# A hybrid attention and state-space layer: first q panel tiles in the row norm, convolution steps one at a time, panel loads at the fifth tile

## The reference

```python
xn = _rmsnorm(x, norm1_w)
proj = xn @ w_in
q, k, v, f_raw, z, xbc, dt_raw, g_att, g_ssm = _split_proj(proj)
...
xbc_c, conv_new = _causal_conv(xbc, conv_past, conv_w, conv_b)   # width 4, then silu
y, h_new = _ssd(xh, dt, A, Bm, Cm, h0)
...
merged = (jax.nn.sigmoid(g_att) * (att.reshape(b, T, ATT_WIDTH) @ w_pa)
          + jax.nn.sigmoid(g_ssm) * (y_ssm @ w_pb))
x = x + merged @ w_out
h = _rmsnorm(x, norm2_w)
x = x + jnp.square(jax.nn.relu(h @ w_up)) @ w_down
```

## Time and profile before

| | |
|---|---|
| median of 3 runs | 2886.76 us |
| profiled execution | 2885.89 us |
| its span | 2884.1 us |
| PE busy | 2737.1 us (95%), 18754 matmuls |
| DVE, ACT, POOL busy | 1577.2, 1022.4, 405.7 us |
| stages (us from the start) | norm to 41, q, k, v to 366, attention from about 404 to 1315, SSD and gates from 1330, branches from 1702, output norm from 2010, MLP from 2131 |

### The profile page before, as it was taken

The page is one execution under the profiler, slowest core; times in us unless marked ns, Lnnn a source line. Parts: engine busy times, 40 slices in busy tenths (PEclk is TensorE's granted clock), DMA queues, the critical chain, the costliest instruction groups (busy, mean ns, idle before and its releaser), DMA issues. The chain is left out here.

```text
span 2884.1 us, 47789 instructions
## 1 busy us (share of the span) xinstructions
PE 2737.1 (95%) x18754; PEld 2658.0 (92%) x18754; DVE 1577.2 (55%) x2867; ACT 1022.4 (35%) x2353; POOL 405.7 (14%) x475
## 2 busy tenths in 40 slices
PE   6998979999999999997999989998989999999999
PEld 5997978989999889887999979998989999999999
DVE  4336337656566565565898864464373444434434
ACT  4223336556666655653434331121231111111110
POOL 0000012212122222222555520000000000000000
PEclk8999999999999999998999999999989999999999
DMA  3222232132232222215888873343221111111112
GB/s 115 90 90 53 79 90 91 43 101 76 67 108 76 66 93 58 84 63 140 205 194 214 201 203 121 112 134 128 65 99 58 45 44 45 44 45 44 48 67 96
DMA packets 334448, 273.31 MB, mean 95 GB/s; under 512 B 95952, under 2 KB 311632, under 8 KB 334096
## 3 DMA queue, kind: packets, MB, share of 16 engines
q1 hardware_dynamic: 334224, 270.25, 32.9%
HBM read 197.90 MB, written 72.28 MB: 94 GB/s over the span
## 5 line engine op out<-in xcount | busy, mean ns | idle before, releaser
L411 PE MATMUL banks<-w_hi,xn_hi 128*128 128x256 f32 x1440 | 407.8, 287 | 8.7 <-DVEq L368 5.0
L411 PE MATMUL banks<-w_lo,xn_hi 128*128 128x256 f32 x1440 | 405.5, 286 | 0.0
L414 PE MATMUL banks<-xn_hi,w_hi 128*128 128x352 f32 x1152 | 379.5, 329 | 0.7 <-ACT att_xs L986 0.7
L414 PE MATMUL banks<-xn_hi,w_lo 128*128 128x352 f32 x1152 | 378.7, 329 | 0.0
L414 PE MATMUL banks<-xn_lo,w_hi 128*128 128x352 f32 x1152 | 378.2, 328 | 0.0
L411 PE MATMUL banks<-w_hi,xn_lo 128*128 128x256 f32 x1280 | 366.3, 286 | 0.0
L411 PEld LDWEIGHTS banks<-w_hi,xn_hi 128*128 128x128 f32 x1440 | 276.7, 192 | 10.6 <-DVEq L368 5.1
L411 PEld LDWEIGHTS banks<-w_lo,xn_hi 128*128 128x128 f32 x1440 | 276.6, 192 | 0.2
L1704 PE MATMUL banks<-h_hi,w_hi 128*128 128x352 f32 x768 | 248.8, 324 | 1.9 <-DVEq L1625 1.9
L1704 PE MATMUL banks<-h_lo,w_hi 128*128 128x352 f32 x768 | 248.6, 324 | 0.0
L1704 PE MATMUL banks<-mlp_uhi,w_hi 128*128 128x352 f32 x768 | 248.6, 324 | 0.0
(11 more groups left out here) (293 smaller groups left out, 6160.8 us busy)
## 6 DMA issues: line engine op xcount, KB each, us to landing
w_raw<-in_w_in SPq DMA_DIRECT2D x44, 1024.0 KB, 5.5
scratch_xbc<-att_co SPq DMA_DIRECT2D x32, 512.0 KB, 2.6
ssd_ab<-scratch_acum SPq DMA_DIRECT2D x64, 256.0 KB, 6.0
br_g<-scratch_gates SPq DMA_DIRECT2D x72, 176.0 KB, 2.8
scratch_gates<-hand_tanh SPq DMA_DIRECT2D x48, 176.0 KB, 5.4
scratch_z<-att_z_stage SPq DMA_DIRECT2D x64, 128.0 KB, 1.9
ssd_xbc<-scratch_xbc SPq DMA_DIRECT2D x64, 128.0 KB, 3.4
ssd_xbc<-scratch_xbc SPq DMA_DIRECT2D x128, 64.0 KB, 3.7
```

The lines of the kernel that those rows point to most:

```text
L411: ins = self.nc.tensor.matmul(self.bank(n, P, PW), x[:, k, t * P:(t + 1) * P], w[:, k, :], start=first, stop=end)
L414: ins = self.nc.tensor.matmul(self.bank(n, P, TT), w[:, k, m * P:(m + 1) * P], x[:, k, r * TT:(r + 1) * TT], start=first, stop=end)
```

## The change

Four things are changed.

1. In `norm_split`, the q panel is loaded before row tile 3, its high part is made by ACT ahead of the sixth squares and its low part by DVE ahead of the seventh round. PE multiplies the first eight tiles of that panel there (`multiply`), each behind the transposes of the tile three further on, and keeps the results in banks 4 to 7 (`held_bank`, two tiles a bank). SP loads the k panel behind it. `project_qkv` begins with the ninth tile; ACT reads the eight held ones from their banks.
2. The load of panel j + 2 is issued after the fifth tile (`t == 4`), in all streams.
3. The low parts of the panels are made by DVE in the attention stage as well; POOL keeps only the doubling copies.
4. The convolution's five instructions of a block are put in a queue (`due`), and `step` runs one of them at given places in a unit; what is left of a block four tiles after its end is run then. ACT's tanh and the stores of the block come one tile later. `share[2]` is (2, 2, 4) where it was (2, 3, 3).

```diff
+HELD = 8
+def held_bank(core, n, rows, cols):
+    b = (5, 6, 7, 4)[n // 2]
+    return core.banks[0:rows, b, (n % 2) * PW:(n % 2) * PW + cols]
...
             for t in range(1, NT):
+                if t == W_AT:
+                    sp.dma_start(panel(core.raw), following...).then_inc(p_loaded, 16)
                 sp.dma_start(rows[:, t, :], srcs[0][t * P:(t + 1) * P, :]).then_inc(loaded[t], 16)
...
+            sp.wait_ge(p_split, 2)
+            sp.dma_start(panel(core.raw), second...).then_inc(next_loaded, 16)
+            sp.wait_ge(next_loaded, 16)
...
-                if t == NT + 1:
+                if t == W_AT + 2:
                     act.wait_ge(p_loaded, 16)
                     nc.scalar.activation(core.whi[0][:], core.raw[:], ACT.Copy).then_inc(p_split, 1)
...
+                if t == W_AT + 3:
+                    dve.wait_ge(p_split, 1)
+                    nc.vector.tensor_tensor(core.wlo[0][:], core.raw[:], core.whi[0][:].bitcast(F32), ALU.subtract).then_inc(p_split, 1)
...
+            def multiply(t):
+                if t == 0:
+                    pe.wait_ge(p_split, 2)
+                pe.wait_ge(lo_made, 2 * t + 2)
+                passes = [(x, w, k) for k in range(KB) for x, w in ((hi, whi), (hi, wlo), (lo, whi))]
...
+                for m in behind(t):          # [t - 3] for t from 3 to 8
+                    multiply(m)
+            for m in range(NT - LAG, HELD):  # 6, 7
+                multiply(m)
+            pe.wait_ge(multiplied, HELD)
...
     def sp(self, sp, i, n, last):
         j, t = self.tiles[n]
-        if t == 5:
+        if t == 4:
             self.load(sp, i, j + 2, last)
...
-        if 1 <= t < 5 and not self.low_on_pool:
-            self.split_lo(dve, self.nc.vector, i, j + 1, t - 1)
+        if 1 <= t < 5:
+            self.split_lo(dve, i, j + 1, t - 1)
...
+        if i == 0 and n < self.held:
+            if n == 0:
+                pe.sem_inc(self.full, self.held)
+            return
...
+            after_held = n - self.held if self.held and i == 0 else 3
+            if after_held < 3:
+                pe.wait_ge(self.free, len(self.banks) + 2 * (after_held + 1))
...
-        stream = Stream(..., 2, (5, 6, 7), ...)
+        stream = Stream(..., 2, (6, 7, 5), ...)
+        stream.held = HELD
...
     def dve(self, dve, i, n):            # ConvFm
+        for k, m in self.ended(n - 4):
+            while self.due and self.due[0][0] <= (i * self.per + k) * 2 + m:
+                self.step(dve)
+        for k, m in self.ended(n):
+            self.due += [((i * self.per + k) * 2 + m, j) for j in range(CW)]
         for k, m in self.ended(n - 5):
+            self.due += [((i * self.per + k) * 2 + m, CW)]
...
-        share = {0: (3, 2, 1), 1: (3, 2, 1), 2: (2, 3, 3), 3: (2, 3, 1), 4: (2, 2, 1)}
+        share = {0: (3, 2, 1), 1: (3, 2, 1), 2: (2, 2, 4), 3: (2, 3, 1), 4: (2, 2, 1)}
...
                 if ngroups[u] == 2:
                     probs_lo(h, u, 1)
+                xbc.step(dve)
                 if x:
                     tile_ends(*units[x - 1], 2)
                 tile_ends(h, u, 0)
...
                 if early(u) and len(nxt) == 2:
                     top_score(hn, nxt[1])
+                    xbc.step(dve)
...
                 tile_ends(h, u, 1)
+                xbc.step(dve)
                 if not early(u) and len(nxt) == 2:
                     top_score(hn, nxt[1])
+                    xbc.step(dve)
                     invert(hn, nxt[1])
...
                 add_out(x)
+                xbc.step(dve)
```

More of the change, by code:

```diff
@@ L14 @@
+from collections import deque
 from contextlib import ExitStack
@@ L236, in _, with behind @@
             nc.vector.tensor_copy(hi[:, :, T:T + TS], lo[:, :, TP:T].bitcast(F32)).then_inc(padded, 1)
-            dve.wait_ge(p_split, 1)
-            nc.vector.tensor_tensor(core.wlo[0][:], core.raw[:], core.whi[0][:].bitcast(F32), ALU.subtract).then_inc(p_split, 1)
         @block.tensor
         def _(pe):
+            whi, wlo = panel(core.whi[0]), panel(core.wlo[0])
+            def multiply(t):
[3 more added lines that the diff above has]
+                passes = [(x, w, k) for k in range(KB) for x, w in ((hi, whi), (hi, wlo), (lo, whi))]
+                for c, (x, w, k) in enumerate(passes):
+                    ins = nc.tensor.matmul(held_bank(core, t, P, PW), x[:, k, t * P:(t + 1) * P], w[:, k, :],
+                                           start=c == 0, stop=c == len(passes) - 1)
+                ins.then_inc(multiplied, 1)
+            def behind(t):
+                return [t - LAG - 1] if LAG < t <= NT else []
             for t in range(NT + 1):
@@ L289, in mine, with bank @@
         return [(self.panels[j][3], t)] if self.panels[j][2] is ep else []
-    def bank(self, n, rows, cols):
+    def bank(self, n, rows, cols, i=1):
+        if i == 0 and n < self.held:
+            return held_bank(self.core, n, rows, cols)
         return self.core.banks[0:rows, self.banks[n % len(self.banks)], 0:cols]
@@ L354, in start_act @@
             ep.start_act(act)
[L356 to L364, removed]
     def start_dve(self, dve):
-        if not self.low_on_pool:
-            dve.sem_inc(self.lo_made, 4)
+        dve.sem_inc(self.lo_made, 4)
         for ep in self.epilogues():
@@ L503, in act @@
             s.wait_full(act, i, n)
[L504 to L505 removed]
+            s.nc.scalar.activation(self.stage[x][0:m, t, :], s.bank(n, m, PW, i), ACT.Copy).then_inc(self.copied, 1)
+            s.nc.scalar.activation(self.sq[0:m, t, :], s.bank(n, m, PW, i), ACT.Square).then_inc(s.free, 1)
     def dve(self, dve, i, n):
@@ L751, in panel @@
             return True, lambda i: w_in[:, bass.ds((2 * i + r) * PW + part * D, PW)], ep, occurrence
-        stream = Stream(core, "tiles", sb, sem, hi, lo, [panel(part, r) for r in range(2) for part in range(3)], 2, (5, 6, 7),
+        stream = Stream(core, "tiles", sb, sem, hi, lo, [panel(part, r) for r in range(2) for part in range(3)], 2, (6, 7, 5),
                         w_in[:, C_X:C_X + PW])
+        stream.held = HELD
         norm.stream = v.stream = stream
@@ L994, in dve @@
     def dve(self, dve, i, n):
[L995 to L1011, removed]
-                    else:
-                        step(s.nc.vector.scalar_tensor_tensor(out=co, in0=xs[:, j:j + L], scalar=self.taps[:, bass.ds(B + j * NB, 1)], in1=co,
-                                                              op0=ALU.mult, op1=ALU.add))
@@ L1021, in sp, with last_tile @@
+    def last_tile(self, B):
+        i, k, m = B // 2 // self.per, B // 2 % self.per, B % 2
+        s = self.stream
+        return i * s.slots + next(n for n, (j, t) in enumerate(s.tiles) if s.panels[j][2] is self and (s.panels[j][3], t) == (k, 3 * m + 2))
     def sp(self, sp, i, n):
-        for k, m in self.ended(n - 5):
+        for k, m in self.ended(n - 6):
             B = (i * self.per + k) * 2 + m
```

76 lines of the change are left out of this document (43 added, 33 removed).

## The result

The changed kernel took **2908.28 us** (median of 4 runs, 2906.98 to 2918.11), the kernel before, on the same chip, 2886.88 (2885.06 to 2887.47). That is 21.4 us slower, where 2855 was forecast. The ratio is 1.0083, 95% interval 1.006 to 1.0105; it is estimated from all the runs and isn't the quotient of the two medians, which would be 1.0074. The profiled execution took 2906.98 us, with a span of 2905.2.

A forecast was written before the change was run, and what follows sets the result against it. PE's own work was taken to bound the attention stage, busy 870 of 911 us. Terms 0.8 - 18.3 - 14 - 8 + 8 = -31.5 gave 2855 us; own range 2842 to 2866, reaching down to 2838.

The forecast's parts named there:

- Part 1: Norm stage: eight tiles multiplied there take 23 us off later, lost again as cover; cost 0.8, bounds 3.5 gained, 16.5 lost.
- rival C: Norm stage: the clock stays at half, costing 16.5 us instead of 0.8; 2871 us, chance 0.12.
- Part 2: Attention stage: panel loads after the fifth tile end late loads, 9.8 us waits plus 8.5 clock; 18.3 less, bounds 0 and 18.3.
- Part 3: Attention stage: low parts moved from POOL to DVE add 66 us to DVE, 27 come back, net 39 more.
- 8 us of new waits: Attention stage: charge for 39 us more DVE work in 80 units, seen where the score path is tight; bounds 0 and 55.
- Part 4: Attention stage: convolution steps run one at a time shorten DVE stretches before the reciprocal; 14 us off, bounds 0 and 21.6.
- rival D: Attention stage: queue and places don't match, most steps come forced at the fourth tile; about 2879 us, chance 0.08.
- The share: Attention stage: a fourth part in the third unit's last slot covers the fourth unit's turn; 8 us off, bounds 4 and 10.
- Rival A: Attention stage: added work makes DVE late on the score path; 2913 us, or 2931 with late loads uncured; chance 0.14.
- two signs that were to show a wrong forecast: Attention stage: DVE's share passing 70%, or PE waiting longer for the scaling than before.

The follow-up runs named there:

- e12: The change with the old convolution steps and the row norm of the kernel before; 1.0 us from e7, within both intervals.
- e7: The change with the convolution steps, tanh and stores of the kernel before; 2876.80 us.
- e4: The kernel before with only the panel load moved to after the fifth tile; 2889.5 us.
- e11: The change with the old convolution steps and the old share (2, 3, 3); 2873.93 us, ratio 0.9949.
- e13: The kernel before with only the attention stage's low parts moved to DVE; 2885.64 us.
- e8: The change with the attention stage's low parts on POOL again; median 7.2 us above the change, intervals overlapping.
- e9: The change with a block's last step writing into the tanh buffer and the store reading it there; 2879.41 us.
- e5: The change with a block's tap steps entering the queue one tile later; slower than the change, attention stage 14.4 us longer.
- e10: The change with the store out of the tanh buffer and the old share (2, 3, 3); 2870.83 us, ratio 0.9945.
- e1: The change with the convolution's stores reading other data of the same size, so first steps wait for no store; 2880.59 us.

## Why the prediction was wrong

**Part 1, tiles in the row norm: right.** Timelines of PE, DVE and ACT, and the windows, which answer to the earlier trace rows:

```profile
27.32 0.58 PE L268 MATMUL banks<-w_hi,xn_hi 128*128 128x256 f32 x1 [1.54 <-DVE w_lo L244]
```

```profile
64.64 0.58 PE L452 MATMUL banks<-w_hi,xn_hi 128*128 128x256 f32 x1 [7.19 <-ACT qkv_sq L546]
...
68.64 0.42 PE L452 MATMUL banks<-w_hi,xn_lo 128*128 128x256 f32 x1
```

```profile
58.81 0.91 DVE L631 MEMSET qkv_dec_w<- 128x1024 f32 x1 [9.22 <-PEq L107]
...
62.56 0.27 DVE L529 MEMSET qkv_sq<- 128x256 f32 x1
```

```profile
62.87 0.38 ACT L545 ACTIVATE qkv_norm_stage<-banks 128x256 f32<-128x256 f32 x1 [13.93 <-DVE qkv_sq L529]
```

```profile
33.20:60.30 27.10, 24.25 (x207) 23.85 (x205) 10.75 (x21) 5.03 (x12) 0.00 (x0) 1.00 0.01 2
60.50:70.50 10.00, 5.86 (x27) 5.86 (x28) 6.32 (x14) 7.20 (x22) 0.00 (x0) 0.50 0.30 53
```

The first product starts at 27.32 (W's low part was said to be done at 28.1), the next stage's memsets at 58.81 (59.9), ACT at 62.87 (63.9), tile 8 at 64.64 (65.7). Tile 9 starts two matmuls ahead of the 68.64, with the clock at 0.5 for two us more; before it was 68.9. The clock was 1.00 from 33.2 to 60.3 in the norm stage, so rival C is out. Said was a cost of 0.8; e12 and e7 show nothing that can be told, so the sum's term isn't contradicted, and isn't confirmed either.

**Part 2, loads at the fifth tile: the size was wrong.** ACT's three waits went, as said. The price of SP's stores behind the load was "1 to 2 us at most, off PE's path". It counted a later issue. It didn't count that the stores then land behind 1 MB, nor that a DVE step on the score path can wait for them, and in e4, with the chunk on POOL, that took the gain. With the chunk on DVE, as the forecast had it, no wait of DVE for a store is left in e7 and e11, so there the price wasn't too low; what was mis-sized is the gain. Of the 18.3 us the load alone gave nothing (e4: from 0.6 us gained to 4.3 lost); with the low parts on DVE it gave 11.7 (e13 to e11, with what the row norm may have in it).

**Part 3, low parts on DVE: right in its terms.** The groups of the attention stage, which answer to the earlier trace rows:

```profile
L1065 DVE SCALAR_TENSOR_TENSOR att_co<-att_xs,att_taps,att_co 128x1059 f32<-128x1059 f32 x96 | 125.9, 1312 | 0.5
...
L385 DVE TENSOR_TENSOR w_lo<-w_raw,w_hi 128x512 fp32r<-128x512 f32 x96 | 67.9, 713 | 0.2
...
L1055 DVE SCALAR_TENSOR_TENSOR att_co<-att_co_tanh,att_co 128x1059 f32<-128x1059 f32 x32 | 40.0, 1250 | 0.6 <-ACT att_co_tanh L1018 0.5
...
L888 DVE SCALAR_TENSOR_TENSOR att_z_stage<-att_z_tanh,att_z_stage 128x256 f32<-128x256 f32 x64 | 26.6, 420 | 35.8 <-ACT att_z_stage L879 35.5
```

The step's mean fell from 1396 to 1312 ns, the gate's from 568 to 420, as said. The chunk has 713 against 689 in the earlier trace rows, and 688 in e13, where the same copies stay on POOL, so they hardly block it. The rule of the Trainium skill ("SBUF — State Buffer", "Who interferes with whom") agrees in these traces on the side of what left POOL; the blocking that it allows for the new chunks is at most 24 ns each. The run e8 fits less well: with the chunks on POOL again the step's mean is 1426, but the gate's only 431. DVE's busy time in e13, 404 to 1315, is 583.8 against 555.3: 28.5 more, where 39 were said. No run shows the 8 us of new waits charged for it: alone it costs nothing (e13), and taking it back out of the change gains nothing (e8, 7.2 us higher, within the intervals).

**Part 4, steps one at a time: the step that failed.** The queue did what was said. Of the 160 steps three follow directly on another in DVE's order, each a first step that then stands for the store, where before there were 46 pairs, 7 triples and 2 fours, so rival D is out. But "Against it new waits: 39 us of DVE work" priced work alone, and no term priced the wait that a block's first step carries, for the store of the block before last.

Before, a block's last step came five tiles after its end and the next first step in the same buffer seven tiles after it (two blocks are six tiles, and one of lag): two tiles of the order, nominally some 11 us. DVE runs tile ends in bunches, though, and the trace of before has 3.04 to 12.0 us between these two steps where no z panel lies between the blocks; twice the store landed only 0.13 us before the first step began (at 797.55, with the first step at 797.68). The wait was closer to biting than the order says. With the queue the first step can come at six tiles, and the store is issued at six instead of five. In the twelve waits the store has landed 2.9 to 8.6 us after the last step's end, where e9's first steps come as little as 0.14 us behind it. The wait itself was there before; the two edits that made it bite are in the change (the tap steps at `ended(n)`, SP's stores at `ended(n - 6)`). Which of the two costs more no run separates: e5 moves the first steps alone, and the last steps moved with them.

Said was -14 and +8; measured against the old steps is +33 (1.0083 and 0.9968), and with the store wait taken away and the old share -3, which can't be told from nothing (e10, e11). The exp's waits that it was to cure were cured by parts 2 and 3 together (2.1, 1.8 and 2.1 us in e7, e11 and e12, against 10.9 and 11.5 with either alone, in e4 and e13).

**The share: wrong sign.** Said was -8. Its cover did take 4 us off the turn, but four parts in one slot end tiles faster than ACT empties their banks: 6 us of bank waits that no term had. Undone, it gained 8.6 with the queue (e10); the 2.9 with the old steps (e11) are within the intervals.

**Rival A had the sign and nearly the time (2913), with another cause.** It made DVE late on the score path by work. DVE was late there by standing still: in e1, e7 and e9 it has the same work, and the loss is gone. That its figure came near the measured one is luck. Of the two signs that were to show a wrong forecast neither came (DVE has 62%, and PE waits 21.2 us for the scaling, less than before): both watched DVE's work and the turn, and the loss came through the exp's waits and the clock.

**The sums.** The terms add up to 2855 as stated. The range's lower end doesn't come out of the bounds named for it: they give 2841 with the 8 us of new waits and 2833 without, where 2838 stands. The chances as listed give 0.82 for faster, 0.06 for same and 0.12 for slower. Neither bears on the outcome.

## What to carry to other kernels

When steps of an in-order engine are moved earlier, list what each waits for, and how far behind its releaser it is in the new order. Read that distance off the trace too: two tiles of the order were 3 to 12 us here, and the wait was worth 28 us once they were gone. A load moved forward has to be checked against every store that it passes in its issuing queue, and against who waits for those stores. Where a buffer's reuse hangs on a store, let the last step write where nobody is in a hurry (here the tanh buffer).

## What the runs showed of the hardware

A small store can land late because of what stands ahead of it. The 16 KB store is issued some 0.4 us behind the 512 KB one on the same queue, and their medians in the change are 2.5 and 2.6 us, so it lands last; how fast it would land alone no run shows. Behind 1 MB it took 8.2 us. In all three waits shown above, the 16 KB store is the last to land, and so the one that a wait lasts for.
